# The last projection by token halves, begun inside attention's last steps

## What is computed

```
h = rmsnorm(x, norm_pre)
pool_u, pool_gate, q, k, v, attn_gate = split(h @ w_in)
pool_out = pool_mixer(pool_u) * silu(pool_gate)                # 512 features, 4 groups of 128
attn_out = swa_sink_attention(q, k, v) * silu(attn_gate)       # 8 heads of 64, 2 k/v heads, window 128
y = concat(pool_out, attn_out) @ w_out                         # 1024 x 1024: the last projection
x = x + rmsnorm(y, norm_post)
```

## Time and profile before

| | |
|---|---|
| median of 3 runs | 2502.53 us (2500.46 to 2507.02) |
| the profiled execution | 2507.68 us, its span 2505.9 us |
| PE busy in the span | 2386.8 us, 95% |
| DVE, POOL, ACT busy | 51%, 30%, 28% |
| mean granted clock of PE | 0.987 |
| attention's opening | 2214.4 to 2248.5 us |
| attention's last two steps | 2366.0 to 2382.4 us |
| last projection | 2382.4 to 2474.2 us |
| from the last product to the end | 31.7 us |

### The profile page before, as it was taken

The page is one execution under the profiler, slowest core; times in us unless marked ns, Lnnn a source line. Parts: engine busy times, 40 slices in busy tenths (PEclk is TensorE's granted clock), DMA queues, the critical chain, the costliest instruction groups (busy, mean ns, idle before and its releaser), DMA issues.

```text
span 2505.9 us, 33582 instructions
## 1 busy us (share of the span) xinstructions
PE 2386.8 (95%) x12944; PEld 1927.5 (77%) x12944; DVE 1277.2 (51%) x1446; ACT 693.3 (28%) x1076; POOL 752.0 (30%) x397
## 2 busy tenths in 40 slices
PE   4999999999999999898999999999999999989895
PEld 3788878887887788787787788888878787767674
DVE  6543353426433543765547644554441487737723
ACT  3422221213213222433233211111132454024421
POOL 1311231122123112113365433333334445312132
PEclk9999999999999999999999999999999999999897
DMA  3211111121112114644444111111124332111011
GB/s 120 72 46 60 60 51 60 44 76 51 51 51 68 59 51 140 227 140 160 176 126 151 52 49 50 42 50 42 50 92 138 114 118 89 54 51 43 26 42 67
DMA packets 59663, 201.01 MB, mean 80 GB/s; under 512 B 6048, under 2 KB 10272, under 8 KB 58912
## 3 DMA queue, kind: packets, MB, share of 16 engines
q1 hardware_dynamic: 39408, 134.56, 17.3%
q10 hardware_dynamic: 20144, 64.80, 7.0%
HBM read 163.16 MB, written 36.18 MB: 80 GB/s over the span
## 4 chain that ended last, share of the span: by engine, by line
PE 80%; DVE 11%; ACT 3%; DVEq 3%; issue 2%; ACTq 0%; DMA 0%; POOL 0%; POOLq 0%
PE psg L446 10%; PE psg L451 10%; PE psg L450 10%; PE psg L579 5%; PE psg L577 5%; PE psg L572 5%; PE psa L669 1%; PE psg L1110 1%; PE psg L1115 1%; PE psb L658 1%; PE psg L1117 1%; PE psa L509 1%; PE psb L665 1%; PE psg L536 1%; DVE rw_SC L1348 1%
## 5 line engine op out<-in xcount | busy, mean ns | idle before, releaser
L387 POOL CAST whi<-wraw 128x1024 fp32r<-128x1024 f32 (+1 forms) x168 | 180.2, 1072 | 1531.5 <-PE psg L572 558.6
L389 POOL TENSOR_TENSOR wlo<-wraw,whi 128x1024 fp32r<-128x1024 f32 (+1 forms) x168 | 443.8, 2642 | 26.2 <-issue 6.3
L446 PE MATMUL psg<-xhi,whi 128*128 128x512 f32 x1120 | 446.7, 399 | 2.0 <-issue 1.6
L451 PE MATMUL psg<-xhi,wlo 128*128 128x512 f32 x1120 | 443.5, 396 | 0.0
L450 PE MATMUL psg<-xlo,whi 128*128 128x512 f32 x1120 | 440.1, 393 | 0.0
L577 PE MATMUL psg<-xlo,whi 128*128 128x512 f32 x640 | 260.6, 407 | 0.0
L579 PE MATMUL psg<-xhi,wlo 128*128 128x512 f32 x640 | 260.6, 407 | 0.0
L572 PE MATMUL psg<-xhi,whi 128*128 128x512 f32 x640 | 258.5, 404 | 0.0
L451 PEld LDWEIGHTS psg<-xhi,wlo 128*128 128x128 f32 x1120 | 210.3, 188 | 52.6
L446 PEld LDWEIGHTS psg<-xhi,whi 128*128 128x128 f32 x1120 | 210.3, 188 | 52.5 <-issue 3.2
L450 PEld LDWEIGHTS psg<-xlo,whi 128*128 128x128 f32 x1120 | 210.3, 188 | 52.2 <-issue 1.0
(11 more groups left out here) (579 smaller groups left out, 4556.9 us busy)
## 6 DMA issues: line engine op xcount, KB each, us to landing
wraw<-w SPq DMA_DIRECT2D x216, 512.0 KB, 3.6
later_scratch<-stage ACTq DMA_DIRECT2D x40, 512.0 KB, 2.6
xres<-xt ACTq DMA_DIRECT2D x4, 1024.0 KB, 10.5
RV<-later_scratch SPq DMA_DIRECT2D x4, 1024.0 KB, 12.0
RG<-later_scratch SPq DMA_DIRECT2D x4, 1024.0 KB, 5.9
later_scratch<-rstage ACTq DMA_DIRECT2D x8, 512.0 KB, 2.6
mgr<-later_scratch ACTq DMA_DIRECT2D x8, 512.0 KB, 3.6
mgt<-later_scratch ACTq DMA_DIRECT2D x8, 512.0 KB, 4.5
```

The source lines that it names most:

```text
L387: pool.tensor_copy(whi[:, u, 0:width], wraw[:, u, 0:width])
L389: pool.tensor_tensor(wlo[:, u, 0:width], wraw[:, u, 0:width], whi[:, u, 0:width].bitcast(F32), ALU.subtract).then_inc(w_ready, 1)
L446: mm = pe.matmul(ps[:, cols], whi[:, slot, w_cols], rhs_hi(k, cols), start=(k == 0), stop=False)
L451: mm = pe.matmul(ps[:, cols], wlo[:, slot, w_cols], rhs_hi(k, cols), start=False, stop=(k == kts - 1))
```

## The change

- The order of the projections becomes k, queries of pair 0, v, then the rest. The values' product is one of those that `fill` issues: 7 matmuls before the first scores, 12 after them, 35 in step 0; there the values are copied, transposed (`turn_values`) and copied again.
- The last projection is made of 16 half blocks (`last_block`): output tile j for tokens 0 to 511, all 8 tiles, then all for tokens 512 to 1023. The weights are loaded and split once for each half. `fill` goes on into it: 24 matmuls in step 14, 38 in step 15 (24 of them ahead of its transposes).
- For that the first half of `cat` has to be split before attention ends: the highs by ACT in steps 13 and 14, the lows of tiles 0 to 2 by POOL and of 3 to 7 by DVE. The last gate is scaled, sent through the sigmoid and applied by halves.
- Squares, sums, root and output tiles are made by half. The first half's lie beside the second half's products.

```diff
-            split_blocks(B_P2, NBLK)
+            split_blocks(B_P2, B_O2)
+            pool.wait_ge(sem("op_high"), SPLIT_BEFORE["cat"] + LOWS_BY_POOL)
+            for j in range(LOWS_BY_POOL):
+                pool.tensor_tensor(xlo[:, j, 0:HALF], cat[:, j, 0:HALF], xhi[:, j, 0:HALF].bitcast(F32), ALU.subtract)
+            split_blocks(B_O2, NBLK)
...
-            later_product(9, 4)
-            pe.wait_ge(g_free[1], T_P2 // 2 + 6)
-            for c in range(NB):
-                mm = pe.transpose(psb[:, c // 4, (c % 4) * P:(c % 4 + 1) * P], kv_f[:, c * P:c * P + P], m(M_ID))
-            mm.then_inc(sem("v2_tr"), 1)
-            pe.wait_ge(sem("v2_ready"), 1)
+            def turn_values():
+                pe.wait_ge(g_free[0], T_P2 // 2 + 7)
+                for c in range(NB):
+                    mm = pe.transpose(psb[:, c // 4, (c % 4) * P:(c % 4 + 1) * P], kv_f[:, c * P:c * P + P], m(M_ID))
+                mm.then_inc(sem("v2_tr"), 1)
...
+            def last_block(n):
+                u, half = n % 2, n // KT
+                ps = psg[n // 2 % 2][:, u * HALF:(u + 1) * HALF]
+                cols = slice(half * HALF, (half + 1) * HALF)
+                pe.wait_ge(w_ready, B_O2 + n + 3)
+                pe.wait_ge(g_free[n // 2 % 2], T_O2 // 2 + 1 + max(0, n // 4 * 2 - 1 + u))
+                for k in range(KT):
+                    w_cols = slice(k * P, (k + 1) * P)
+                    if n == KT:
+                        pe.wait_ge(sem("op_split"), SPLIT_BEFORE["cat"] + KT - LOWS_BY_POOL + k + 1)
+                    elif n == 0 and k >= LOWS_BY_POOL:
+                        pe.wait_ge(sem("op_split"), SPLIT_BEFORE["cat"] + k - LOWS_BY_POOL + 1)
+                    mm = pe.matmul(ps, whi[:, u, w_cols], xhi[:, k, cols], start=(k == 0), stop=False)
+                    if k == 0:
+                        mm.then_inc(w_used, 1)
+                    yield
+                    pe.matmul(ps, whi[:, u, w_cols], xlo[:, k, cols], start=False, stop=False)
+                    yield
+                    mm = pe.matmul(ps, wlo[:, u, w_cols], xhi[:, k, cols], start=False, stop=(k == KT - 1))
+                    if k == KT - 1:
+                        mm.then_inc(g_full, 1)
+                    yield
+            later = itertools.chain(*(projection(n) for n in range(8)), *(last_block(n) for n in range(KT)))
+            def fill(k):
+                for _ in range(k):
+                    next(later, None)
+            fill(7)
+            pe.wait_ge(sem("kv_ready"), 1)
             scores(0)
+            fill(12)
             for p in range(PAIRS):
-                queries_next = projection(query_at(p + 1)) if p + 1 < PAIRS else iter(())
-                later = itertools.chain(queries_next, projection(gate_at(p)))
-                def fill(k):
-                    for _ in range(k):
-                        next(later, None)
                 for st in range(4):
                     n = 4 * p + st
                     if n + 1 < 4 * PAIRS:
                         scores(n + 1)
-                    fill(10)
+                    if n == 0:
+                        fill(35)
+                        turn_values()
+                        fill(6)
+                        pe.wait_ge(sem("kv_ready"), 2)
+                    else:
+                        fill(24 if n == 4 * PAIRS - 1 else 10)
                     pe.wait_ge(sem("ap_ready"), n + 1)
                     pe.wait_ge(sem("ao_out"), n + 1)
                     for q in range(4):
@@ -1167,11 +1207,31 @@
                                                vt2[:, 2 * st + b + kb, (p // 2) * CH:(p // 2) * CH + CH],
                                                apt[:, 2 * h + b, kb, :], start=(kb == 0), stop=(kb == 1))
                     mm.then_inc(sem("ao_full"), 1)
-                    fill(8)
-            streamed(B_O2, T_O2, sem("op_split"), SPLIT_BEFORE["cat"])
-            plain(B_O2, T_O2, KT // 2, 1)
-            norm_factor(q2acc, q2rstd, "fin")
+                    fill(6 if n == 4 * PAIRS - 3 else 8)
+            for _ in later:
+                pass
+            def last_sums(h):
+                pe.wait_ge(sem("fin_added"), KT * h + KT)
+                for c in range(NB // 2):
+                    t = h * HALF + c * P
+                    mm = pe.matmul(psa[:, h, c * CH:c * CH + CH], q2acc[:, t:t + P], id2[:, :], start=True, stop=True)
+                mm.then_inc(sem("norm_tot"), 1)
+            for _ in last_block(KT):
+                pass
+            last_sums(0)
+            for _ in last_block(KT + 1):
+                pass
+            pe.wait_ge(sem("norm_exp"), NORM["fin0"] + 1)
+            half_spread(0, q2rstd[:, 0:HALF])
+            for n in range(KT + 2, 2 * KT):
+                for _ in last_block(n):
+                    pass
+            last_sums(1)
+            pe.wait_ge(sem("norm_exp"), NORM["fin1"] + 1)
+            half_spread(1, q2rstd[:, HALF:T])
...
+            def last_gate_in(h):
+                cols = half_cols(h)
+                if h:
+                    v.wait_ge(g_full, T_P2 + 18)
+                else:
+                    v.wait_ge(sem("as_full"), 4 * PAIRS - 1)
+                tt(psg[1][:, cols], psg[1][:, cols], rs2[:, cols], MUL).then_inc(sem("ag_in"), 1)
...
                 mm.then_inc(sem("as_out"), 1)
+                if n == 4 * PAIRS - 1:
+                    cat_low(0, KT - 1)
...
                     if p + 1 < PAIRS:
                         queries(p + 1)
                     else:
-                        gate_scaled(p)
+                        cat_low(0, 3)
+                        cat_low(0, 4)
                 if n == 4 * PAIRS - 1:
-                    cat_low(0)
-                    cat_low(1)
+                    last_gate(1).then_inc(g_free[1], 1)
...
+                if n == 4 * PAIRS - 3:
+                    last_gate_in(0)
+                if n == 4 * PAIRS - 2:
+                    cat_low(0, 5)
+                    cat_low(0, 6)
+                    last_gate(0)
+                    last_gated(0)
+                    last_gate_in(1)
+                if n == 0:
+                    v.wait_ge(g_full, T_P2 + 11)
+                    tt(kv_f[:, :], psg[0][:, :], rs2[:, :], MUL).then_inc(g_free[0], 1)
             attended(4 * PAIRS - 1)
-            cat_low(4)
-            cat_low(5)
-            gate_applied(PAIRS - 1)
-            cat_low(6)
-            cat_low(7)
-            start_sum("fin", q2acc)
-            with v.Fori(0, KT // 2) as i:
-                for u in range(2):
+            last_gated(1).then_inc(sem("ao_out"), 1)
+            for j in range(KT):
+                cat_low(1, j)
...
+            for n in range(KT):
+                last_square(n)
+            last_root(0)
+            last_square(KT)
             for j in range(KT):
-                stt(y2[:, j, :], y2[:, j, :], par_col("g2_post", j), flat(psa), MUL, MUL).then_inc(sem("y_scaled"), 1)
-                if j not in BY_POOL:
-                    v.drain()
-                    tt(y2[:, j, :], y2[:, j, :], h2[:, j, :], ADD).then_inc(sem("y_done"), 1)
+                last_tile(0, j)
+                if j in (1, 3, 5, 7):
+                    last_square(KT + 1 + j // 2)
+            for n in (5, 6, 7):
+                last_square(KT + n)
+            last_root(1)
+            for j in range(KT):
+                last_tile(1, j)
...
+                if n == 4 * PAIRS - 3:
+                    s.wait_ge(sem("pool_done"), 4)
+                    s.wait_ge(sem("as_full"), 4 * PAIRS - 1)
+                    cat_high(0, 0, LOWS_BY_POOL)
...
+                    s.wait_ge(g_free[0], T_P2 // 2 + 10)
+                    cat_high(0, 5, 7)
+                    last_sigmoid(0)
...
+                if n == 4 * PAIRS - 3:
+                    cat_high(0, LOWS_BY_POOL, 5)
+                if n == 4 * PAIRS - 2:
+                    s.wait_ge(sem("ag_in"), PAIRS + 1)
+                    cat_high(0, KT - 1, KT)
+                    last_sigmoid(1)
+            s.wait_ge(g_full, T_P2 + 18)
+            cat_high(1, 0, KT - 1)
```

More of the change, by code:

```diff
@@ L267, in build @@
         aq = tiles("aq", 21, [P, 2, T])
-        kv_f, kk_f = tiles("kv_f", 21, [P, T]), tiles("kk_f", 22, [P, T])
+        kv_f, kk_f = tiles("kv_f", 15, [P, T]), tiles("kk_f", 22, [P, T])
         rs2 = drstd
@@ L2154, in _ @@
             s.dma_start(oh[0][:, :, :], xt[:, :, 0:HALF]).then_inc(sem("res_in"), 16)
-            def evacuate(t0, name, y, sq):
-                with s.Fori(0, KT // 2) as i:
-                    for u in range(2):
-                        s.wait_ge(sem(name + "_added"), 2 * i + u + 1)
-                        s.wait_ge(g_full, t0 + 2 * i + u + 1)
-                        s.sem_inc(go, 1)
-                        act(sq[:, u, :], psg[u][:, :], SQ).then_inc(sem("tile_sq"), 1)
-                        act(y[:, bass.ds(2 * i + u, 1), :].rearrange("p a t -> p (a t)"), psg[u][:, :], CP
-                            ).then_inc(g_free[u], 1)
```

(31 more changed lines are left out.)

107 lines of the change are left out of this document (69 added, 38 removed).

## The result

The kernel after took 2479.76 us, median of 4 runs (2478.15 to 2481.46), beside 2504.48 us (2500.46 to 2507.02, 4 runs) for the kernel before: a ratio of 0.9903, 95% interval 0.989 to 0.9915. That is 24.7 us less, where 33.4 were forecast. It lies just inside the upper end of the wide range, 2459 to 2480, and 4.8 us above the forecast's own band, 2464 to 2475.

A forecast was written before the change was run, and what follows sets the result against it. PE was taken as the bound, busy 95%, with gains only where it stands or runs slowly. Opening -12.6, closing -7.3 and tail -13.5 gave -33.4 us: 2469 from 2502.53, forecast 2464 to 2475, 8 in 10 within 2459 to 2480.

The forecast's parts named there:

- What bounds the kernel: Whole kernel: PE busy 95%, time only where it stands or runs slowly; steps between attention's opening and closing unchanged.
- The opening: Attention's start up to the third scores: every PE wait covered by matmuls at full clock, -12.6 us.
- The closing: Last scores to last product: output matmuls fill steps 14 and 15, waits 6.2 us; -7.3 us (-11.9 to -1.6).
- The half blocks: Last projection: new weights every 5.6 us instead of 11.2, kept at pace; 0 us (0 to +10).
- rival 2: Last projection: POOL can't keep the half blocks' pace, 10 us lost over 14 blocks, 2479 us; chance 0.07.
- rival 5: Last projection: weight loads landing late make it slower than before, 2511 us at a 13 us landing; chance 0.03.
- The tail: After the last product: only half the tokens remain, 18.3 against 31.8 us; -13.5 us (-15.5 to -10.7).
- the opening's bound: Attention's start: gain of only 8 us if waits of 1.3 and 1.6 us stay and the clock falls again.
- rival 4: Attention's end and after: waits hardly appear (1.6 us), tail at its lower end; -40 us, 2462 us; chance 0.08.
- rivals 1: Steps 14 and 15: POOL and DVE block each other in the worse order, waits 14.3 us, 2477 us; chance 0.18.
- 3: Attention's start: covered only in part (values' turn, bias or keys late), half the gain, -6.3, 2475 us; chance 0.06.
- The rule weighed: Attention's last steps: two-input DVE and GpSimd operations share ports, first keeps them; without disturbance the sum would be -38.0 us.

The follow-up runs named there:

- alone: The kernel before with only the changed opening (values' product issued by fill, queries first), step 0's last fill at 6: 2495.31 us, 0.9962.
- both holds: Changed kernel, POOL's five weight splits in steps 1 to 12 and the second output block's split each held until that step's softmax is normalised: 2472.59 us, 0.9871.
- step 14's split held: Changed kernel with POOL's split of the second output block held until step 14's softmax is normalised: 2482.88 us, 0.9913.
- the lead alone: The kernel before with attention's projections in one sequence and step 0's last fill raised from 8 to 10 matmuls: 2511.99 us, 1.0026.

## Why the prediction was right and wrong

**What bounds the kernel, failed.** "No idle PE there; those steps keep their length." The rows of before did show a full PE, but the step was read as if nothing acted on it, and its change was put at 0. It was +6.4 us, of the 7.0 by which the sum over the stages missed. The shift was in the prediction's own terms (a lead of 2 matmuls was counted, as a gain for the closing), and so was the hazard: the earlier trace rows were used for the closing alone. What wasn't asked is which of POOL and DVE starts first in each later step, though before's margin could have been read: in a step of its trace the normalising, then POOL's cast, stand at

```profile
2295.05 1.23 DVE L1911 TENSOR_TENSOR ap__181<-ap__181,sm 128x1024 f32<-128x1024 f32 x1
```

```profile
2295.06 2.12 POOL L387 CAST whi<-wraw 128x1024 fp32r<-128x1024 f32 x1 [13.26 <-PE psg L1110]
```

0.01 us apart. The lead gave back 0.47 us in step 13, and cost 6.4.

**The opening, right but 0.8 us too much.** The forecast was -12.6; it gave -11.8 in the change and alone. No wait of PE is left there and the clock is 1.00. The third scores came 14.4 us earlier; less the 3.0 of the untouched part, 11.4. Of the 0.8 us some 0.6 is the price of changing between kinds of work, which had no term, and 0.2 a slip in adding (below):

```profile
2378.58 0.40 PE L1167 MATMUL psg<-xhi,wlo 128*128 128x512 f32 x1
2378.90 1.09 PE L1206 MATMUL psb<-apt,vt 128*64 128x128 f32 x16
2379.93 0.50 PE L1161 MATMUL psg<-xhi,whi 128*128 128x512 f32 x1
2380.26 0.39 PE L1165 MATMUL psg<-xlo,whi 128*128 128x512 f32 x1
```

These are PE's rows around the last step's products, kernel after. From start to start two projection matmuls lie 0.23 us apart; the one ahead of the products and the one behind take 0.32 and 0.33, so this group costs 1.2 us and not 1.02. Before's step had shown it: its 3.35 us of attention's own are 0.4 more than scores, transposes and products by their rows, 1.06, 0.87 and 1.02.

**The closing, right in its sum, in part by luck.** -7.3 forecast, -7.2 measured. Within it the idle waits were 3.7 us where 4.8 were put: 3.0 on step 14's transposes (2.3 put, cause as given), 0.7 on POOL's first split (1 put), none on step 15's (1 put) and none on the last subtraction (0.5 put). The clock cost 1.3 (1.4 put): from start to start 0.77 on the transposes and 0.5 on the three matmuls after them, which took 0.57, 0.43 and 0.29. The last 1.2 us had no term: they are the same changes between kinds of work, some 0.1 us at each of about a dozen places. So 1.1 us of waits too many stood against 1.2 us that were left out. With both holds the same count gives 1.6 us, with 3.2 of waits.

**The half blocks, right.** They ran at pace: 46.50 us busy of 46.5, one each 5.6 us, no wait on POOL or a DMA there; the loads landed in 3.6 us in the median over the run. Rivals 2 and 5 fall.

**The tail, right.** The forecast was -13.5, the measurement -13.8. The chain of waits after the last product:

```profile
2458.55 0.61 ACT q2sq L2556
...
2463.45 0.75 DVE y L2039
...
2473.38 0.69 DVE y L2043
```

That is 4.9 us to the first tile (5.2 put), 10.6 of tiles (10.2) and 2.4 to the end (2.9); before, took 9.5, 19.2 and 3.1.

**Slips in the working.** None of them made the miss of 6.4 us. A granted clock of 0.90 over 34.1 us is 6.8 us at half clock and 3.4 lost, not 3.4 and 1.7, so the opening's bound would have been about -6, not -8. The opening's terms with their hops add up to 21.8 us, not 21.6. The lower ends of the closing's waits add up to 0.6 us, not 1.6, so its bound and rival 4 lie 1 us further out. And PE's waits in before's closing were 8.5 us, not 6.3: 2.2 on ACT's copies were left out.

**The rivals.** The time came out near rivals 1, 3 and 2 (2477, 2475, 2479), and none of them is what happened: the closing and the opening each gave about what was forecast. Rival 1 named the right mechanism, POOL and DVE in the worse order, in the wrong steps. The rule weighed was right in kind. The Trainium skill, SBUF — State Buffer, section "Who interferes with whom", lets whichever starts first keep the ports whole; the rows agree, in both directions: 3.28 us of normalising when POOL is 0.21 us ahead, 2.12 us of cast when DVE is first.

## What to carry to other kernels

Before moving work on the engine that sets the pace, follow what it triggers: here PE's start of a block releases POOL, and which of POOL and DVE comes first decides whether their meeting costs PE nothing or 1.3 us (6.4 over five). Where two engines meet within a few tenths of a microsecond, a shift of 2 matmuls elsewhere can turn the order over in every step; an explicit wait of the one with slack on the one without set it here and cost PE nothing. Where the engine has no slack at any place, though, an ordering only moves the hold to the next operation: in the closing 3.0 us of wait became 2.3 and then 2.1, and of what was tried only less work on POOL took it away.

## What the runs showed of the hardware that was not expected

- The hold is nearly the whole operation: a normalising of 1.22 us took 3.28 beside a subtraction of 2.40 that was 0.21 us ahead. Turned about, the same two engines' meeting cost PE nothing.
- It reaches operations on 4 elements: in step 14 they took 0.90, 0.92 and 0.99 us rather than the 0.17 of their like (the earlier trace rows had such cases). The first ends with POOL's subtractions, the other two with its cast, which has one input; one of them (line 1972) is a tensor-scalar form, the others take two.
- The cast is held in its turn: 2120 ns beside the normalising, 1039 alone.
- The granted clock fell by the end of the wait of 3.0 us: the eight transposes after it took 1.97 us and not 1.09, and the next matmul 0.78 rather than 0.47. It stayed at 1.00 behind the 2.3 us with step 14's split held, and behind the 1.1 us in steps 1 to 12. But the length of a wait doesn't settle it: the same wait in the same place, 1.88 us in before and 1.87 in the kernel with the lead alone, was followed by slow transposes in the one and by full pace in the other:

```profile
2367.96 1.97 PE L1158 MATMUL psb<-mat,ap__181 128*128 128x128 f32 x8 [1.88 <-DVE ap__181 L1911]
```

```profile
2374.61 1.09 PE L1157 MATMUL psb<-mat,ap__181 128*128 128x128 f32 x8 [1.87 <-DVE ap__181 L1910]
```
